# Hybrid MLA and RWKV-7 encoder on one core: centred values, squares from the banks, four more banks for the turned probabilities

## The reference, cut

```python
for l in range(DEPTH):                                     # 2 layers
    x = x + 0.5 * _swiglu(_rms_norm(x, ffn1_norm[l]), ...)  # d_ff 2816
    p = _rms_norm(x, mix_norm[l]) @ w_in[l]
    y_mla  = _mla(p[..., :MLA_IN], ...)      # 8 heads, chunk-causal softmax over 256 keys
    y_rwkv = _rwkv7(p[..., MLA_IN:], ...)
    y = concatenate([_rms_norm(y_mla, out_norm_mla[l]), _rms_norm(y_rwkv, out_norm_rwkv[l])])
    x = x + y @ w_out[l]
    x = x + 0.5 * _swiglu(_rms_norm(x, ffn2_norm[l]), ...)

# _rwkv7, per head of 64:
state = state * w_t + (state @ a_t) b_t^T + v_t k_t^T ;  y_t = state @ r_t
mean = jnp.mean(y, -1); var = jnp.mean((y - mean) ** 2, -1)
y = (y - mean) * lax.rsqrt(var + GN_EPS) * gn_gain + gn_bias
bonus = sum(r * k * r_k) * v
y = (y + bonus) * g                          # g: gate from a low-rank projection
```

## Time and profile before

| | |
|---|---|
| median of three runs | 1172.84 us (1170.21 to 1175.96) |
| profiled execution | 1172.02 us, span 1170.0 us |
| TensorE busy | 1146.7 us of the span |
| VectorE busy | 800.0 us |
| ScalarE busy | 562.2 us |
| mean granted TensorE clock | 0.993 of full |
| tail of layer 0, first turned probability to turn of x | 354.39 to 398.17 us |
| tail of layer 1 | 930.21 to 975.27 us |

### The profile page before, as it was taken

One profiled execution on the slowest core, in us unless ns is written; L12 is line 12 of the kernel. 1 busy time (PEld: TensorE's weight loads), 2 busy tenths in 40 slices (PEclk: granted clock), 3 DMA queues, 4 the chain that ended last, 5 costly groups with the idle time before them and its releaser, 6 DMA issues.

```text
span 1170.0 us, 27236 instructions
## 1 busy us (share of the span) xinstructions
PE 1146.7 (98%) x10724; PEld 1060.7 (91%) x10724; DVE 800.0 (68%) x1462; ACT 562.2 (48%) x995; POOL 2.1 (0%) x11
## 2 busy tenths in 40 slices
PE   7999999999999999999999999999999999999998
PEld 6999999999978899999989999989999788999997
DVE  4666666888645876666686666677885568666665
ACT  4444444596233544444454444456843345444443
POOL 0000000000000000000000000000000000000000
PEclk8999999999999999999999999999999999999999
DMA  6666665754000466666556666666530014766663
GB/s 188 198 183 191 182 183 170 186 141 128 4 2 8 137 196 182 183 189 183 179 163 184 187 186 183 187 166 161 145 92 4 3 54 133 201 188 180 186 190 126
DMA packets 243958, 173.41 MB, mean 148 GB/s; under 512 B 14428, under 2 KB 228596, under 8 KB 243892
## 3 DMA queue, kind: packets, MB, share of 16 engines
q1 hardware_dynamic: 243892, 172.46, 50.5%
HBM read 171.39 MB, written 1.05 MB: 147 GB/s over the span
## 4 chain that ended last, share of the span: by engine, by line
PE 82%; DVE 11%; ACT 4%; issue 1%; DMA 1%; SPq 0%; ACTq 0%; DVEq 0%
PE bank L1352 23%; PE bank L1353 23%; PE bank L1354 23%; PE bank L1365 9%; DVE wlo L808 2%; DVE xlo L837 1%; PE bank L1359 1%; ACT whi L530 1%; PE bank L1491 1%; DMA raw<-in_ffn_w_gate_dram 1%; ACT work L645 0%; DVE xtok L1323 0%; PE bank L1490 0%; PE bank L1665 0%; DVE work L977 0%
## 5 line engine op out<-in xcount | busy, mean ns | idle before, releaser
L808 DVE TENSOR_TENSOR wlo<-raw,whi 128x1024 fp32r<-128x1024 f32 (+1 forms) x322 | 392.5, 1221 | 241.7 <-ACT whi L530 241.2
L1352 PE MATMUL bank<-xhi,whi 128*128 128x256 f32 x1696 | 484.3, 286 | 6.0 <-DVE xlo L837 5.3
L1354 PE MATMUL bank<-xhi,wlo 128*128 128x256 f32 x1696 | 480.4, 283 | 0.0
L1353 PE MATMUL bank<-xlo,whi 128*128 128x256 f32 x1696 | 480.4, 283 | 0.0
L530 ACT ACTIVATE whi<-raw 128x1024 fp32r<-128x1024 f32 (+1 forms) x322 | 338.8, 1052 | 293.0 <-PE bank L1354 258.3
L1352 PEld LDWEIGHTS bank<-xhi,whi 128*128 128x128 f32 x1696 | 325.6, 192 | 13.1 <-issue 7.8
L1353 PEld LDWEIGHTS bank<-xlo,whi 128*128 128x128 f32 x1696 | 325.7, 192 | 3.7 <-issue 0.5
L1354 PEld LDWEIGHTS bank<-xhi,wlo 128*128 128x128 f32 x1696 | 325.6, 192 | 0.0
L1352 PE MATMUL bank<-whi,hhi 128*128 128x512 f32 x352 | 138.7, 394 | 1.1 <-DVE hlo L923 1.0
L1353 PE MATMUL bank<-wlo,hhi 128*128 128x512 f32 x352 | 138.0, 392 | 0.0
L1354 PE MATMUL bank<-whi,hlo 128*128 128x512 f32 x352 | 137.0, 389 | 0.0
(11 more groups left out here) (223 smaller groups left out, 1033.5 us busy)
## 6 DMA issues: line engine op xcount, KB each, us to landing
raw<-in_ffn_w_gate_dram SPq DMA_DIRECT2D x88, 512.0 KB, 3.9
raw<-in_ffn_w_up_dram SPq DMA_DIRECT2D x88, 512.0 KB, 3.9
raw<-in_ffn_w_down_dram SPq DMA_DIRECT2D x88, 512.0 KB, 3.5
raw<-in_w_in_dram SPq DMA_DIRECT2D x32, 512.0 KB, 3.9
raw<-in_w_out_dram SPq DMA_DIRECT2D x16, 512.0 KB, 3.6
raw<-in_w_q_up_dram SPq DMA_DIRECT2D x4, 384.0 KB, 3.2
xtok<-in_x_dram SPq DMA_DIRECT2D x4, 256.0 KB, 5.4
raw<-in_w_in_dram SPq DMA_DIRECT2D x4, 256.0 KB, 4.3
```

Of the source, the lines that this page charges most:

```text
L808: V_.tensor_tensor(wlo[:, b.slot, 0:width], raw[:, b.slot, 0:width], whi[:, b.slot, 0:width].bitcast(F32), ALU.subtract).then_inc(lo_ready, 1)
L1352: mm(out, hi, mhi, start=start, stop=False, **kw)
L1353: mm(out, hi, mlo, start=False, stop=False, **kw)
L1354: return mm(out, lo, mhi, start=False, stop=stop, **kw)
```

## The change

- The values of RWKV are centred: the matmul that turns them to token order takes `centre` (the identity less 1/64) in place of `eyes`. As y is linear in the values, y comes without its mean, and the mean's matmuls and subtraction are dropped.
- ScalarE squares y straight out of banks 0 and 1, in two halves (`squared_y`), and the variance is summed in two halves of eight passes, into bank 0.
- ScalarE copies each gate tile a second time, multiplied by `gn_gain` (`gain_gT`). VectorE's `kept_y` multiplies y by it while copying, four 256-wide instructions; both halves come after the loop over the chunks.
- VectorE makes (bonus + `gn_bias`) * gate ahead of the tail's waits (`bg`, four instructions). The steps `gg` and `gm` are dropped: what is left is `gy`, now four instructions into `yN`, and `gb`.
- The six tiles of turned probabilities go to banks 6, 7, 5, 6, 7, 1; the attention products to banks 4 and 5, then 6 and 7.
- ScalarE makes the RWKV high parts ahead of the split of `out5`.

```diff
-for _name, _k in [..., ("eyes", 64), ("upper", 128),
+for _name, _k in [..., ("eyes", 64), ("centre", 64), ("upper", 128),
+    put("centre", (row == col) - np.float32(1 / HEAD))
...
+    bonus, gain_gT = unit(15), unit(1)
...
                 def kept_gate(i):                                   # ScalarE
                     act.wait_ge(mix_pe.sem, mix_pe.at(l, f"gup_{i}"))
-                    nc.scalar.activation(gT[:, SEQ * i:SEQ * (i + 1)], bank[7][:, SEQ * (i % 2):SEQ * (i % 2 + 1)],
-                                         ACT.Copy).then_inc(mix_act.sem, mix_act.step(f"gT{i}"))
+                    out = bank[7][:, SEQ * (i % 2):SEQ * (i % 2 + 1)]
+                    nc.scalar.activation(gT[:, SEQ * i:SEQ * (i + 1)], out, ACT.Copy)
+                    nc.scalar.activation(gain_gT[:, SEQ * i:SEQ * (i + 1)], out, ACT.Copy,
+                                         scale=col("gn_gain", i)).then_inc(mix_act.sem, mix_act.step(f"gT{i}"))
...
+                def squared_y(b):
+                    if b:
+                        act.wait_ge(mix_dve.sem, mix_dve.at(l, "ye1"))
+                    else:
+                        act.wait_ge(mix_pe.sem, mix_pe.at(l, "y1"))
+                    nc.scalar.activation(ysc[:, 512 * b:512 * (b + 1)], bank[b][:],
+                                         ACT.Square).then_inc(mix_act.sem, mix_act.step(f"gsq{b}"))
...
                 kept_gate(3)
+                squared_y(0)
                 kept_prob(0)
                 exps(3)
-                act.wait_ge(mix_dve.sem, mix_dve.at(l, "yc"))
-                nc.scalar.activation(ysc, yT, ACT.Square).then_inc(mix_act.sem, mix_act.step("gsq"))
+                squared_y(1)
                 kept_prob(3)
...
-                ahead(out0 + 3), ahead(out0 + 4), ahead(out0 + 5)
-                act.wait_ge(mix_dve.sem, mix_dve.at(l, "gm"))
+                ahead(out0 + 3), ahead(out0 + 4)
+                act.wait_ge(mix_dve.sem, mix_dve.at(l, "gb"))
                 for j in range(HP):
                     nc.scalar.activation(xhi[:, 4 + j, :], yN[:, SEQ * j:SEQ * (j + 1)], ACT.Copy,
                                          scale=col("out_norm_rwkv", j)).then_inc(...)
+                ahead(out0 + 5)
...
                 def kept_y(b):                                      # VectorE
                     dve.wait_ge(mix_pe.sem, mix_pe.at(l, f"y{2 * b + 1}"))
-                    V_.tensor_copy(yT[:, 512 * b:512 * (b + 1)], bank[b][:]).then_inc(mix_dve.sem, mix_dve.step(f"ye{b}"))
+                    dve.wait_ge(mix_act.sem, mix_act.at(l, "gT3" if b else "gsq0"))
+                    for c in (2 * b, 2 * b + 1):
+                        ins = V_.tensor_tensor(yT_c[:, c], bank[b][:, 256 * (c % 2):256 * (c % 2 + 1)].rearrange(
+                            "p (h i) -> p h i", h=HP), chunked(gain_gT)[:, c], ALU.mult)
+                    ins.then_inc(mix_dve.sem, mix_dve.step(f"ye{b}"))
...
-                    if c % 2:
-                        kept_y(c // 2)
+                kept_y(0), kept_y(1)
                 for i in (1, 2): ...                                # probability copies
-                dve.wait_ge(mix_pe.sem, mix_pe.at(l, "mean"))
-                for b in range(2):
-                    s = slice(512 * b, 512 * (b + 1))
-                    ins = V_.tensor_tensor(yT[:, s], yT[:, s], bank[4 + b][:], ALU.subtract)
-                ins.then_inc(mix_dve.sem, mix_dve.step("yc"))
+                dve.wait_ge(mix_dve.sem, mix_dve.at(l, "bonus1"))
+                dve.wait_ge(mix_act.sem, mix_act.at(l, "gT3"))
+                for j in range(HP):
+                    ins = V_.scalar_tensor_tensor(tiles(bonus, j), tiles(bonus, j), col("gn_bias", j), tiles(gT, j), ALU.add,
+                                                  ALU.mult)
+                ins.then_inc(mix_dve.sem, mix_dve.step("bg"))
...
-                for b in range(2):
-                    ins = V_.tensor_tensor(yT[:, s], yT[:, s], bank[6 + b][:], ALU.mult)
+                for c in range(NC):
+                    spread = bank[6 + c // 2][:, 256 * (c % 2):256 * (c % 2 + 1)].rearrange("p (h i) -> p h i", h=HP)
+                    ins = V_.tensor_tensor(chunked(yN)[:, c], yT_c[:, c], spread, ALU.mult)
                 ins.then_inc(mix_dve.sem, mix_dve.step("gy"))
+                ahead(out0 + 3)
                 dve.wait_ge(mix_dve.sem, mix_dve.at(l, "gy"))
-                for j in range(HP):
-                    ins = V_.tensor_scalar(tiles(yN, j)..., y_h[:, j], col("gn_gain", j), col("gn_bias", j), ALU.mult, ALU.add)
-                ins.then_inc(mix_dve.sem, mix_dve.step("gg"))
-                ahead(out0 + 3)
+                dve.wait_ge(mix_dve.sem, mix_dve.at(l, "bg"))
                 V_.tensor_tensor(yN, yN, bonus, ALU.add).then_inc(mix_dve.sem, mix_dve.step("gb"))
-                V_.tensor_tensor(yN, yN, gT, ALU.mult).then_inc(mix_dve.sem, mix_dve.step("gm"))
                 ahead(out0 + 4)
...
-                                ins = both(out[:, 64 * j:64 * (j + 1)], src, eyes, True, True)
+                                ins = both(out[:, 64 * j:64 * (j + 1)], src, con("centre") if name == "tv" else eyes, True, True)
...
+                TURNED = (6, 7, 5, 6, 7, 1)                          # TensorE
                 def turned_prob(i):                                 # waits: ex1, gT3, u3, pT0, pT1, then gsq1 and ye1
...
+                def variances(b):
+                    pe.wait_ge(mix_act.sem, mix_act.at(l, f"gsq{b}"))
+                    pe.wait_ge(mix_dve.sem, mix_dve.at(l, "ye0"))
+                    for j in range(4 * b, 4 * b + 4):
+                        ins = mm(bank[0][:, 2 * j:2 * j + 2], ysc[:, P * j:P * (j + 1)], con("meanbd")[:, 0:P:64],
+                                 start=True, stop=True)
+                    return ins
                 turned_prob(0), turned_prob(1), turned_prob(2)
-                pe.wait_ge(mix_dve.sem, mix_dve.at(l, "ye1"))
-                for b in range(2):
-                    ins = mm(bank[4 + b][:], con("meanbd"), yT[:, 512 * b:512 * (b + 1)], start=True, stop=True)
-                ins.then_inc(mix_pe.sem, mix_pe.step("mean"))
+                variances(0)
                 ...                                                 # attended(0..3), fillers, turned_prob(3..5)
-                for j in range(8): ...                              # variance, bank 4
+                variances(1).then_inc(mix_pe.sem, mix_pe.step("var"))
...
+                pe.wait_ge(mix_dve.sem, mix_dve.at(l, "gv"))
                 output(0)
```

More of the change, by code:

```diff
@@ L80 @@
 _n = 0
-for _name, _k in [("ident", 128), ("ones", 128), ("onesbd", 128), ("meanbd", 128), ("eyes", 64), ("upper", 128),
+for _name, _k in [("ident", 128), ("ones", 128), ("onesbd", 128), ("meanbd", 128), ("eyes", 64), ("centre", 64), ("upper", 128),
                   ("level", LEVELS * 64), ("level1T", 64), ("reset", 256), ("cos", 32), ("sin", 32), ("tail", 1)]:
@@ L1269, in mixing @@
                 dve.wait_ge(mix_pe.sem, mix_pe.at(l, "var"))
-                V_.tensor_scalar(root[:, 0, 0:16], bank[4][:, 0:16], GN_EPS, None,
+                V_.tensor_scalar(root[:, 0, 0:16], bank[0][:, 0:16], GN_EPS, None,
                                  ALU.add).then_inc(mix_dve.sem, mix_dve.step("gv"))
@@ L1618, in fill @@
                                 src = {"tb": bC[:, g, :], "tk": kC[:, g, :], "tv": vT_g[:, g // HP, g % HP, :]}[name]
-                                ins = both(out[:, 64 * j:64 * (j + 1)], src, eyes, True, True)
+                                ins = both(out[:, 64 * j:64 * (j + 1)], src, con("centre") if name == "tv" else eyes, True,
+                                           True)
                         if name[0] == "Q":
@@ L1716, in mixing @@
                         bonus_sum(c)
+                TURNED = (6, 7, 5, 6, 7, 1)
                 def turned_prob(i):
                     b, m = i // 3, i % 3
+                    if i == 0:
+                        pe.wait_ge(mix_act.sem, mix_act.at(l, "ex1"))
                     if i == 1:
                         pe.wait_ge(mix_act.sem, mix_act.at(l, "gT3"))
-                    if i > 1:
-                        st = mix_dve if i in (3, 4) else mix_act
-                        pe.wait_ge(st.sem, st.at(l, f"pT{i - 2}"))
-                    if i == 0:
-                        pe.wait_ge(mix_act.sem, mix_act.at(l, "ex1"))
+                    if i == 2:
+                        pe.wait_ge(mix_dve.sem, mix_dve.at(l, "u3"))
+                    if i == 3:
+                        pe.wait_ge(mix_act.sem, mix_act.at(l, "pT0"))
+                    if i == 4:
+                        pe.wait_ge(mix_dve.sem, mix_dve.at(l, "pT1"))
+                    if i == 5:
+                        pe.wait_ge(mix_act.sem, mix_act.at(l, "gsq1"))
+                        pe.wait_ge(mix_dve.sem, mix_dve.at(l, "ye1"))
                     for j in range(4):
```

(8 more changed lines are left out.)

30 lines of the change are left out of this document (11 added, 19 removed), and 2 rows, old and new, of the table MIX_P.

## The result

The kernel after takes 1165.91 us (median of seven runs, 1163.23 to 1167.34) against 1172.84: a ratio of 0.9942, 95% interval 0.9925 to 0.9959. That is 1.3 us above the predicted 1164.6, inside the range, and 0.58% faster than before; the interval leaves out a ratio of 1. The profiled execution took 1167.3 us (span 1165.3), 4.7 less than the profiled one of before.

What follows compares the result with a forecast made beforehand. TensorE, busy 98% of the span, bounds the kernel; vector work matters only where it waits. Layer 0 gains 3.52 us, layer 1 4.79, less 0.1 at the start: 8.2, so median 1164.6 us, range 1162.6 to 1166.6.

Steps and rivals of the forecast that it cites:

- The front: Tail up to output block 1: earlier attention products 0.50, turned-probability banks 0.31, shorter variance 0.85, together 1.66 us a layer.
- dear bound: VectorE's four 256-wide products of y with the gate at 0.69 us each, 2.76 in all; front then gains 0.4.
- the cheap bound: VectorE's four 256-wide products of y with the gate cost 1.50 us, priced by the nearest row, L1262.
- rival 2: VectorE piles up: strided gate halves cost 0.69 us each, not 0.375, giving 1167.1 us; chance 0.11.
- The end: Product with the spread root to turn of x: 23.68 us becomes 21.82, gain 1.86 a layer, clock included.
- rival 4: End of tail: RWKV high parts wait for ScalarE, block 7 starts no earlier, front alone gains, 1168.3 us; chance 0.05.
- Layer 1's clock: Layer 1's extra clock fall ahead of its first output block doesn't return, gaining 1.27 us more than layer 0.
- Rival 1: Low clock level moves into each layer's thinned stretch, 1.5 us a spell; 1169.1 us, or 1167.6 or 1170.4; chance 0.20.
- Rival 3: Low level holds from the thinned stretch to the root's spread, 13.8 us slower, 1186.6 us; chance 0.04.
- The rule of the Trainium skill: Transposes don't bring TensorE's full rate; against the change, as layer 1's row would lose 1.3 us a layer there.
- The start: Kernel start: constants grow by 32 KB on 704.5 KB, costing at most 0.2 us, taken as 0.1.
- Costed at nothing: ScalarE's squares and second gate copies, VectorE's bias times gate and new waits: hidden behind idle time or other work.

Runs made afterwards that it cites:

- the last version: Kernel after with probability copies ahead of y's second half, block 8's low part ahead of the RWKV root, and two filler matmuls: 1160.56 us, ratio 0.9899.

## Why the prediction was right, point by point

**The front, predicted 1.66 us a layer, measured 14.85 - 12.79 = 2.06 in layer 0.** Both are the time to output block 1. The products start at 2.76 us after the first turned probability (predicted 3.06): VectorE is the last, as said, by 0.45 us, and its instructions overlap by 0.08 each, which the sum of durations left out; four products took 1.42 (predicted 1.50, dear bound 2.76), two copies 1.28 (1.38). So the cheap bound held, and rival 2 is out. From the products' end to the end of the variance 1.36 us went (predicted 0.31 + 0.85 = 1.16): the banks gave 0.49 where I put 0.31, as the idle of 0.25 cost more than its row; the other 0.87 goes with the variance's eight fewer passes (predicted 0.85), which no run undid alone. The products themselves lost 0.11 to their start after an idle. The prediction's "up to 2.0" was the better figure.

**The end, predicted 1.86 us a layer, measured 1.84 in layer 0 and in layer 1.** Here gy is the start of the product with the spread root. Block 7 starts at gy + 15.15 with no idle (predicted 15.39), VectorE ready at 387.87, gy + 14.22 (predicted 14.08), an idle of 0.80 ahead of block 8 (predicted about 1), x turned at gy + 21.84 and 21.82 (predicted 21.82). The step that carried this, that the root of the RWKV norm waits for the one-column passes and takes block 8's low parts with it, is confirmed by moving those low parts: 1.10 us more a layer. ScalarE's order is needed: without it 0.79 of the 1.84 is lost, which is rival 4's mechanism at less than half of its price. The two vector steps dropped are worth 1.23 a layer in the kernel after. The spell after the one-column passes stands in both layers of the kernel before in both its profiles, and in neither layer of the kernel after in either of its own. Of the other kernels the one with ScalarE's order undone has it, in layer 1; there the idle ahead of block 7 is back. None of the 18 tails in which block 7 follows without an idle has it, but neither do the two with the vector steps put back, where the idle is 1.10 again. So that the gain came as added up rests on about 1.0 us of work, which is the 1.10 that the prediction gave for the case that the low level comes back, and about 0.8 us of clock, whose cause the runs don't settle.

**Layer 1's clock, predicted a gain of 1.27 us, measured a loss.** This is the term that failed. I took it that the fall would not return, as the thin stretch ahead of it got shorter. It came earlier, in the middle of the first attention products, for 6.8 us in one profile and 3.4 in the other: 3.31 and 1.70 us lost, where before lost 1.27, so 2.0 and 0.4 worse instead of 1.27 better. Rival 1 had the mechanism (the low level moves), at 1.5 us a spell, close to the 1.70 of the shorter one, but put one in each layer; it was layer 1 alone, and not in the traces of all kernels with this front. Rival 3 had the low level hold through all thin stretches of both layers; the longest spell of these kernels was 6.8 us, in one layer. The rule of the Trainium skill that I weighed ("TensorE: Matmul & The Clock Gate", section "Part 4: PE-mode transpose") says that transposes don't bring the full rate. The traces agree only so far that the level fell behind such a stretch (0.57 from 931 to 939); the twelve transposes of layer 0, 1.47 us of them in a row, ran at a granted 1.00. It didn't fall there in the three traces with dense work added (fillers twice, the mean's passes), but neither did it in the six of the other kernels with the changed front, nor ever in layer 0. What decides between the executions, and whether the transposes, the two-column passes or the idle carry it, stays open: one execution of each kernel was traced, and the three weren't tried apart.

**The sum.** Layer 0 gave 3.90 us (predicted 3.52); layer 1 without a spell would give 3.90 + 1.28 = 5.2 (predicted 4.79), together 9.1 for 8.2, and 1172.84 - 9.1 = 1163.7. The run of 1163.23 at 0.997 fits that; both profiled ones have a spell in layer 1, and most runs stand near them, at 1165.6 to 1167.4 and 0.992 to 0.994. So the median's nearness to the forecast is in part two errors against each other: the front 0.4 a layer too small, layer 1's clock 1.7 to 3.3 too good.

**The start, predicted -0.1, profiled -1.22.** Two traces of the kernel before reach the first turned probability at 354.39 and 355.21, the eleven of kernels with the changed front at 354.34 to 356.00. A cost of the change at the start can't be read from this scatter. It does not lie in the mixing stage: from the turn of x in layer 0 to the first turned probability of layer 1 it takes 532.04 us before and 531.97 after.

**Costed at nothing, and so it was.** By the same 531.97 the second gate copies and the first squares cost nothing in layer 1's loop. ScalarE's squares and gate copies end no wait of TensorE or VectorE in layer 0's tail; bias times gate took 1.67 us (358.23 to 359.90), inside the 2.7 of cover.

## What to carry to other kernels

When a wait goes, name the next one by the row that will release it, and price its removal as well: here the low part behind the norm's root was in the prediction as "about 1 us idle", and moving one line gave 1.10 us a layer on top of the 1.84 of the change's whole end. A timed gain of half a per cent can be work or clock; compare runs at a like granted clock, or the tails' lengths in the traces, before crediting an edit. Whether dense matmuls left out between thin ones are paid back in clock isn't settled here: the clock fell there in both traces of the kernel after and in none of the other nine. Where the next engine forces an idle anyway, fillers in it cost nothing to try (the products start at +2.77 with and without them).

## What the runs showed of the hardware that was not expected

The granted clock of one stretch, with the same instructions ahead of it, differs between executions and between layers. Around the attention products of layer 1 the low level took 6.8 and 3.4 us in the two traces of the kernel after and none in nine others with the changed front; in the kernel before it took 3.4 us twice, and 10.2 with one unused constant more. TensorE was busy all through the spell of 6.8 us; the idle ahead of the products it fell in was 0.45 us.

A kernel's times go with its mean clock: before from 1169.98 us at 0.994 to 1176.44 at 0.987, after from 1163.23 at 0.997 to 1167.34 at 0.992. Six runs of the last version spread over 0.9 us, five of the same without fillers over 2.25.

An idle can cost more than its row says: removing idle rows of 0.80 and 0.25 us shortened the tail by 1.10 and 0.49 us.
